# Attention's small matmuls on a full array, and the rotary part of two heads on separate halves of its rows

## The reference, cut to what matters

```
q_pe = rope(q[..., NOPE_DIM:], pos_f)                  # NOPE_DIM = 128, ROPE_DIM = 64
kv = (ckv_all @ w_ukv).reshape(B, Lk, MLA_HEADS, NOPE_DIM + V_DIM)
k_nope, v = kv[..., :NOPE_DIM], kv[..., NOPE_DIM:]
s = jnp.einsum('bqhd,bkhd->bhqk', qn, k_nope) + jnp.einsum('bqhr,bkr->bhqk', qp, k_pe)
s = s.astype(F32) * scale
s = jnp.where(k_chunk[None, :] <= qc[:, None], s, -jnp.inf)
p = jax.nn.softmax(s, axis=-1).astype(v.dtype)
return jnp.einsum('bhqk,bkhv->bqhv', p, v)
```

## Time and profile before

| | |
|---|---|
| median of 3 runs | 2828.89 us (2827.05 to 2829.56) |
| the profiled execution | 2828.93 us |
| its span, first to last instruction | 2827.1 us |
| TensorE busy | 2713.4 us, 96% of the span |
| VectorE busy | 1811.6 us, 64% |
| ScalarE busy | 1252.4 us, 44% |
| mean granted clock of TensorE | 0.982 of full speed |
| share of TensorE in the chain that ended last | 89% |

### The profile page before, as it was taken

One profiled execution on the slowest core, in us unless ns is written; L12 is line 12 of the kernel. 1 busy time (PEld: TensorE's weight loads), 2 busy tenths in 40 slices (PEclk: granted clock), 3 DMA queues, 4 the chain that ended last, 5 costly groups with the idle time before them and its releaser, 6 DMA issues.

```text
span 2827.1 us, 56045 instructions
## 1 busy us (share of the span) xinstructions
PE 2713.4 (96%) x20006; PEld 2675.8 (95%) x20006; DVE 1811.6 (64%) x3039; ACT 1252.4 (44%) x2039; POOL 452.9 (16%) x856
## 2 busy tenths in 40 slices
PE   6999999988999999999999899997999999999997
PEld 6999999987999999999999888897999999999997
DVE  6677777757666644666655754447766644666655
ACT  5555555534444433444434445434444433444432
POOL 3111111002222200222200200002322200222200
PEclk9999999989999999999999899998999999999999
DMA  5434444433444455545455332243444555544553
GB/s 199 133 124 133 139 138 132 135 103 116 152 165 164 154 172 168 165 164 166 146 176 169 119 93 78 87 136 116 153 166 163 164 165 167 165 163 165 160 165 114
DMA packets 124256, 413.58 MB, mean 146 GB/s; under 512 B 14032, under 2 KB 22384, under 8 KB 124176
## 3 DMA queue, kind: packets, MB, share of 16 engines
q1 hardware_dynamic: 116064, 406.37, 44.8%
q10 hardware_dynamic: 7056, 3.21, 0.4%
q0 software_dynamic: 1056, 2.92, 0.3%
HBM read 406.97 MB, written 5.48 MB: 146 GB/s over the span
## 4 chain that ended last, share of the span: by engine, by line
PE 89%; DVE 7%; ACT 1%; issue 1%; DMA 1%; POOL 0%; SPq 0%; DVEq 0%; ACTq 0%; POOLq 0%
PE bank L223 28%; PE bank L225 27%; PE bank L224 27%; DVE X L836 1%; DVE h_lo L841 1%; PE bank L633 1%; DVE Y L832 1%; PE bank L629 1%; DMA raw<-in_w_hi_in 1%; PE bank L594 1%; DVE Y L555 1%; PE bank L1361 0%; DVE Y L553 0%; POOL ssx L816 0%; PE bank L603 0%
## 5 line engine op out<-in xcount | busy, mean ns | idle before, releaser
L223 PE MATMUL bank<-h_hi,w_hi 128*128 128x288 f32 (+1 forms) x4208 | 1280.2, 304 | 71.4 <-DVE h_lo L841 46.4
L224 PE MATMUL bank<-h_lo,w_hi 128*128 128x288 f32 (+1 forms) x4208 | 1257.4, 299 | 0.0
L225 PE MATMUL bank<-h_hi,w_lo 128*128 128x288 f32 (+1 forms) x4208 | 1253.4, 298 | 0.0
L210 ACT ACTIVATE w_hi<-raw 128x1024 fp32r<-128x1024 f32 (+2 forms) x786 | 808.5, 1037 | 954.8 <-PE bank L225 939.5
L217 DVE TENSOR_TENSOR w_lo<-raw,w_hi 128x1024 fp32r<-128x1024 f32 (+2 forms) x786 | 940.9, 1207 | 424.2 <-ACT w_hi L210 423.9
L223 PEld LDWEIGHTS bank<-h_hi,w_hi 128*128 128x128 f32 x4208 | 797.6, 190 | 84.9 <-issue 41.1
L224 PEld LDWEIGHTS bank<-h_lo,w_hi 128*128 128x128 f32 x4208 | 799.4, 190 | 1.8
L225 PEld LDWEIGHTS bank<-h_hi,w_lo 128*128 128x128 f32 x4208 | 800.8, 190 | 0.2
L223 PE MATMUL bank<-g_hi,w_hi 128*128 128x288 f32 x1408 | 416.8, 296 | 0.0
L224 PE MATMUL bank<-g_lo,w_hi 128*128 128x288 f32 x1408 | 415.4, 295 | 0.0
L225 PE MATMUL bank<-g_hi,w_lo 128*128 128x288 f32 x1408 | 413.9, 294 | 0.0
(11 more groups left out here) (243 smaller groups left out, 2255.2 us busy)
## 6 DMA issues: line engine op xcount, KB each, us to landing
raw<-in_w_fi SPq DMA_DIRECT2D x352, 512.0 KB, 4.0
raw<-in_w_hi_in SPq DMA_DIRECT2D x128, 512.0 KB, 4.2
raw<-in_w_fo SPq DMA_DIRECT2D x128, 512.0 KB, 3.5
raw<-in_w_fo SPq DMA_DIRECT2D x64, 384.0 KB, 3.2
raw<-in_w_ho SPq DMA_DIRECT2D x32, 512.0 KB, 4.2
raw<-in_w_mo SPq DMA_DIRECT2D x32, 512.0 KB, 3.9
raw<-in_w_down SPq DMA_DIRECT2D x18, 512.0 KB, 4.5
raw<-in_w_ukv SPq DMA_DIRECT2D x16, 512.0 KB, 3.7
```

Source lines behind the costliest of these rows:

```text
L210: act.activation(w_hi[:, ch.slot, 0:n], raw[:, ch.slot, 0:n], ACT.Copy).then_inc(hi_done, 1)
L223: pe.matmul(out, w_hi[:, ch.slot, w], rhs_hi, start=start, stop=False)
L224: pe.matmul(out, w_hi[:, ch.slot, w], rhs_lo, start=False, stop=False)
L225: return pe.matmul(out, w_lo[:, ch.slot, w], rhs_hi, start=False, stop=stop)
```

## The change

It does the following, for each pair of heads:

- The sample scores take 128 queries as the stationary operand (the last 96 prompt queries and the 32 sample queries), so that the results of the sample queries stand on partitions 96 to 127 (`LAST`). Maxima, exponentials, sums and the division of the sample part work on these partitions.
- The sample scores of head 1 go to bank 4 instead of bank 6. TensorE waits before the scores for the outputs of both heads of the previous pair (`o_done` at 2r + 2, before 2r + 1).
- The scores are issued with the six products over the 128 plain features first, and then the six rotary products, the two heads in turn. The rotary product of head 0 runs over rows 0 to 63 alone and that of head 1 over rows 64 to 127 alone, and the zeros in `qr` (L1105) are no longer written.
- The two small transposes in `turn` are of 128 x 128. The second takes the last 128 of the 160 columns and goes to bank 6 or 4. Transposing the values, the fourth tile is 128 wide too.
- The last product of `outputs` runs over all 128 rows, of which the first 96 meet values of zero. VectorE writes these zeros once (four memsets, after the latent of the queries is split).

```
-        SS = psum[6]
+        SS = [psum[6], psum[4]]
+        LAST = slice(P - TS, P)
@@ down_dve
-            for n in range(2):
-                dve.memset(qr[n], 0.0)
@@ pair_act
-                    act.activation(pt_s[n][:, 0:TS], SC[n][:, 3 * P:3 * P + TS], ACT.Copy)
-                    act.activation(pt_s[n][0:TS, TS:2 * TS], SC[n][0:TS, 3 * P + TS:3 * P + 2 * TS], ACT.Copy)\
-                        .then_inc(m["p_tok"], 1)
+                    act.activation(pt_s[n][:, 0:TS], SC[n][:, 4 * P - TS:4 * P], ACT.Copy)
+                    act.activation(pt_s[n][:, TS:2 * TS], SS[n][:, 4 * P - TS:4 * P], ACT.Copy).then_inc(m["p_tok"], 1)
...
-                    act.activation(pr[n][0:TS, 3 * P:PR], SS[0:TS, n * 160:n * 160 + 160], ACT.Exp, bias=nb[0:TS, n, 2:3],
-                                   scale=SCALE, accum_out=sums[0:TS, n, 2:3]).then_inc(m["probs"], 1)
+                    act.activation(pr[n][LAST, 3 * P:PR], SS[n][LAST, 0:160], ACT.Exp, bias=nb[LAST, n, 2:3],
+                                   scale=SCALE, accum_out=sums[LAST, n, 2:3]).then_inc(m["probs"], 1)
@@ pair_pe
-                    pe.transpose(bank[:, 3 * P:3 * P + TS], pr[n][0:TS, 3 * P:4 * P], ident[0:TS, 0:TS])
-                    pe.transpose(bank[0:TS, 3 * P + TS:3 * P + 2 * TS], pr[n][0:TS, 4 * P:PR], ident[0:TS, 0:TS])\
+                    pe.transpose(bank[:, 3 * P:4 * P], pr[n][:, 3 * P:4 * P], ident[:])
+                    pe.transpose(SS[n][:, 3 * P:4 * P], pr[n][:, PR - P:PR], ident[:])\
                         .then_inc(m["p_turned"], 1)
...
-                    pe.matmul(bank[:, TP:T], vt[n][0:TS, 3 * P:4 * P], pt_s[n][0:TS, TS:2 * TS], start=False,
-                              stop=True).then_inc(m["o_raw"], 1)
+                    pe.matmul(bank[:, TP:T], vt[n][:, 3 * P:4 * P], pt_s[n][:, TS:2 * TS], start=False, stop=True).then_inc(m["o_raw"], 1)
...
-                    w = P if c < 3 else TS
-                    tr = pe.transpose(VT[n][0:w, c * P:(c + 1) * P], vf[n][:, c * P:c * P + w], ident[:])
+                    at = c * P if c < 3 else TK - P
+                    tr = pe.transpose(VT[n][:, c * P:(c + 1) * P], vf[n][:, at:at + P], ident[:])
...
             if attn:
-                pe.wait_ge(m["o_done"], 2 * r + 1)
+                pe.wait_ge(m["o_done"], 2 * r + 2)
+            parts = [(0, P, slice(0, P), slice(0, P)), (P, 3 * P, slice(P, TP), slice(0, TP)),
+                     (0, TK - TP, slice(T - P, T), slice(TP, TK))]
             for n in range(2):
-                for c0, q0, k0, kn_ in ((0, 0, 0, P), (P, P, 0, TP)):
-                    out = SC[n][:, c0:c0 + kn_]
-                    pe.matmul(out, qn[n][:, q0:q0 + P], kn[n][:, k0:k0 + kn_], start=True, stop=False)
-                    pe.matmul(out, qr[n][:, q0:q0 + P], kpe[:, k0:k0 + kn_], start=False, stop=True)
-                out = SS[0:TS, n * 160:n * 160 + 160]
-                pe.matmul(out, qn[n][:, TP:T], kn[n][:, TP:TK], start=True, stop=False)
-                pe.matmul(out, qr[n][:, TP:T], kpe[:, TP:TK], start=False, stop=True).then_inc(m["scores"], 1)
+                for part, (c0, c1, qs, ks) in enumerate(parts):
+                    bank = (SC, SC, SS)[part][n]
+                    pe.matmul(bank[:, c0:c1], qn[n][:, qs], kn[n][:, ks], start=(part != 1), stop=False,
+                              skip_group_check=True)
+            for part, (c0, c1, qs, ks) in enumerate(parts):
+                for n in range(2):
+                    bank, h = (SC, SC, SS)[part][n], slice(64 * n, 64 * n + 64)
+                    sc = pe.matmul(bank[:, c0:c1], qr[n][h, qs], kpe[h, ks], start=False, stop=True, skip_group_check=True)
+                    if part == 2:
+                        sc.then_inc(m["scores"], 1)
@@ the block of VectorE
                     dve.wait_ge(m["out_dma"], 48)
+                    dve.wait_ge(m["cq_ready"], LATENT)
+                    for n in range(2):
+                        dve.memset(vt[n][0:P - TS, 3 * P:4 * P], 0.0)
+                        dve.memset(pr[n][0:P - TS, 3 * P:PR], 0.0)
```

More of the change, by code:

```diff
@@ L1221, in pair_act @@
                     act.activation(vt[n][:, 0:3 * P], VT[n][:, 0:3 * P], ACT.Copy)
-                    act.activation(vt[n][0:TS, 3 * P:4 * P], VT[n][0:TS, 3 * P:4 * P], ACT.Copy).then_inc(m["v_tok"], 1)
+                    act.activation(vt[n][LAST, 3 * P:4 * P], VT[n][LAST, 3 * P:4 * P], ACT.Copy).then_inc(m["v_tok"], 1)
             hi(3)
@@ L1244, in pair_dve @@
                     dve.tensor_tensor(pr[n][:, 0:3 * P], SC[n][:, 0:3 * P], chunk_mask[:], ALU.add).then_inc(m["masked"], 1)
-                    dve.tensor_reduce(mx[0:TS, n, 2:3], SS[0:TS, n * 160:n * 160 + 160], AX_X, ALU.max)
+                    dve.tensor_reduce(mx[LAST, n, 2:3], SS[n][LAST, 0:160], AX_X, ALU.max)
                     dve.wait_ge(m["masked"], 2 * r + n + 1)
@@ L1257, in pair_dve @@
                         dve.tensor_scalar(pr[n][:, c0:c0 + cn], pr[n][:, c0:c0 + cn], rc[:, n, tile:tile + 1], None, ALU.mult)
-                    dve.tensor_scalar(pr[n][0:TS, 3 * P:PR], pr[n][0:TS, 3 * P:PR], rc[0:TS, n, 2:3], None, ALU.mult)\
+                    dve.tensor_scalar(pr[n][LAST, 3 * P:PR], pr[n][LAST, 3 * P:PR], rc[LAST, n, 2:3], None, ALU.mult)\
                         .then_inc(m["normed"], 1)
```

## The result

The changed kernel takes 2811.24 us (2807.63 to 2813.8, four runs) against 2828.22 us for the kernel before on the same chip; the ratio is 0.9939, with a 95% interval from 0.9922 to 0.9956. Timed once more on another occasion, it took 2811.84 against 2828.46, ratio 0.9931 (0.9918 to 0.9945). The forecast, 2814.4, is a ratio of 0.9949: the direction and the kind of gain are right, the size is too small, and the median lies at the lower edge of the range. The profiled execution spans 2810.1 us, 17.0 less than before.

What follows compares the result with a forecast made beforehand. TensorE's own pace was taken to bound the attention step. Savings of 0.97 (scores), 0.36 (`turn`) and 0.48 (`outputs`) make 1.81 us a pair, 14.5 over eight: 2828.9 to 2814.4 us, 8-in-10 range 2811 to 2822.

Steps and rivals of the forecast that it cites:

- TensorE's row sets the step: Attention loop: TensorE is busy throughout the 23.87 us step, so shortening its instructions shortens the step, except just ahead of the scores.
- The rotary products: Scores: the two heads' halves work side by side, 1.2 us instead of 1.84; whole scores 3.47 us, saving 0.97 a pair.
- The visit to the 64-row form: Scores: one visit to this array form, not in the trace, priced at 0.32 us, bounds 0 and 0.65.
- `turn` and `outputs`: Wide forms bring `turn` with its follow-up to 0.74 us and `outputs` to 0.57, saving 0.36 and 0.48 a pair.
- The value transposes: Ahead of the scores: they become wide and may finish sooner, but nothing counted, since TensorE then waits for ScalarE.
- The new wait: Before the scores: waiting for head 1's outputs too costs nothing, its low part being done 1.4 us earlier.
- The memsets: VectorE: four take about 0.65 us, at most 1.2, and fall into 0.87 us in which VectorE waits.
- What comes next: After the scores: they still end after VectorE's weight split, and the softmax finishes 1.5 us before `turn`.
- keep their number and size: Softmax and copies: ScalarE's and VectorE's operations on the sample rows were taken as unchanged.
- One after another: Rival, rotary products: halves don't overlap, only narrow forms are saved, 1.17 us a pair; 2819.5 us, chance 0.25.
- a change for each head: Rival, rotary products: each of five head changes costs 0.16 us, nothing overlaps, 0.37 us saved a pair; 2826 us, chance 0.08.
- loads in the open: Rival, rotary products: weight loads no longer hide, up to 0.19 us an instruction, so slower; 2837.8 us, chance 0.05.

Runs made afterwards that it cites:

- `same_half`: Changed kernel with both heads' rotary products on rows 0 to 63, zeros written again: step 22.84 us against 21.91; 2820.88 us in one run.
- `head_blocks`: Changed kernel with the three rotary products of head 0 issued first, then those of head 1: step 22.25 us against 21.91; 2814.98 us in one run.
- the two narrow experiments: Changed kernel with each head's last `outputs` product, or first small `turn` transpose, on 32 rows again: steps 22.36 and 22.34 us; 2813.44 and 2815.52 us.
- `full_softmax`: Changed kernel with the sample part's maximum, exponential and division over all 128 partitions: step 21.91 us; 2809.49 us, ratio 0.9938 to the kernel before the change.

## Why the prediction was right or wrong

*TensorE's row sets the step.* Right: what the edits added to TensorE's row, 0.34 to 2.87 us, appeared in the step.

*The rotary products.* This is the step that failed. The mechanism, side by side, was right, and its size was off: I let a head's two instructions, the order of issue and the twelve weight loads bind, and took 1.2 us. The rows show two starts at a time and 0.92 us, the bound that I named and set aside. That is 0.28 us a pair, 2.2 us in all. The row that I chose the mechanism by was misread, too: L1286 and L1287, 0.09 us apart, both work on rows 0 to 31, so they say nothing of different rows, for products or for loads. From the traces alone the choice was open, and that it came out was in part luck. The Trainium skill ("TensorEngine Tiling (Array Packing)", Key Properties) says that different tiles load weights and multiply in parallel; `same_half` and the changed kernel agree, 1.84 against 0.92 us. The Trainium skill's page "TensorE: Matmul & The Clock Gate", Part 3, says that matmuls are never reordered in their starts; `head_blocks` has a product on the idle half starting ahead of one issued before it, and there the measurement decides.

*The visit to the 64-row form.* 0.39 us instead of 0.32, which takes back 0.6 us of the 2.2. With the first point, 3.47 - 0.28 + 0.07 = 3.26 us for the scores; measured 3.29.

*`turn` and `outputs`.* Right to 0.01 us each, and the two narrow experiments bring 0.43 and 0.45 us of them back, one by one.

*The value transposes.* Right: the scores start 0.97 us after them, before 0.96, since the evacuation hasn't moved.

*The new wait.* Right: head 1's low part is done at 1691.55 + 0.46 = 1692.01 in the changed kernel, 1.3 us before the scores, and no wait for it stands in the trace.

*The memsets.* Right: the four take 0.66 us (1640.62 to 1641.28, forecast 0.65), and the weight split behind them starts 2.35 us after VectorE begins the latent's split, 2.42 before.

*What comes next, and "keep their number and size".* Wrong, though it cost only some 0.2 us, once, in the last step. I priced the operations on the sample rows by their shapes. On partitions 96 to 127 they no longer overlap with their neighbours, on ScalarE too, here before and then changed:

```profile
1697.30 0.50 ACT L1221 ACTIVATE Y<-bank 128x384 f32<-128x384 f32 x1
1697.67 0.26 ACT L1222 ACTIVATE Y<-bank 32x128 f32<-32x128 f32 x1
1697.83 0.47 ACT L1221 ACTIVATE Y<-bank 128x384 f32<-128x384 f32 x1
```

```profile
1693.15 0.50 ACT L1219 ACTIVATE Y<-bank 128x384 f32<-128x384 f32 x1
1693.66 0.27 ACT L1220 ACTIVATE Y<-bank 32x128 f32<-32x128 f32 x1
1693.96 0.49 ACT L1219 ACTIVATE Y<-bank 128x384 f32<-128x384 f32 x1
```

Before, they start 0.37 and 0.16 us apart; now 0.51 and 0.30, each behind the end of the one ahead. With both heads ScalarE's split comes 0.54 us later after the first score. VectorE's split ends at 1697.06, behind the scores (1696.50) and not ahead of them, so that the mask starts 0.4 us later than it could, and the chain behind is 0.86 us longer. Of 1.5 us of cover, 0.3 are left: the division ends at 1703.13 for a `turn` at 1703.41. `full_softmax` gives back only what the chain had lost: its cover is 1.0 us, for the copies on ScalarE stay as they are. The Trainium skill has the rule ("VectorE: DVE Perf Modes", "Two Vector instructions with no wait between them"): an instruction whose operands start in another group of 32 partitions than the last ones is held until all before it have finished. VectorE's rows agree, 0.58 against 0.47 us. I had not brought it to bear.

*The rivals.* One after another, a change for each head, and loads in the open are excluded by the twelve starts in 0.92 us. The profiled span also has 1.3 us that no step of the sum holds, behind the attention, where the lower clock lasted less long.

## What to carry to other kernels

Small matmuls on a part of the array cost by the change of form, here 0.2 to 0.4 us for a visit: widen them with operands that are there anyway, and if a form is wanted for working side by side, group it so that it is visited once and the two halves alternate. When rows are moved to other partitions for TensorE's sake, price the other engines' neighbours too, for shapes don't show it: what was 1.5 us of cover is 0.3 afterwards. And measure a change of this size by the length of the loop's step, which repeats to 0.02 us where the whole kernel scatters by several.

## What was not expected of the hardware

Products on different halves start together even if each head's second instruction is issued ahead of the other head's first, and an idle half takes a product ahead of two issued before it, one still running and one not begun (`head_blocks`, 1.25 us for the rotary part against 0.92 and 1.84). VectorE's operations on partitions 96 to 127 between operations on all 128, and those behind them, start 0.09 to 0.12 us later than the same operations over all partitions. ScalarE's copies on partitions 96 to 127, and those behind them, start 0.14 us later than such copies on partitions 0 to 31; over all partitions that wasn't run.
